# PE's branch around the further expert passes: the last position first, a copy of it behind the passes

## The reference

```
def moe_ffn(x, w_router, router_bias, w_gate, w_up, w_down):
    ...                                  # each token picks 2 of 16 experts, with weights
    h = silu(einsum("td,edf->tef", t, w_gate)) * einsum("td,edf->tef", t, w_up)
    h = h * gates[..., None]
    return einsum("tef,efd->td", h, w_down)
x = x + g2 * moe_ffn(h, ...)
y = rmsnorm(x, norm_final)
```

## Time and profile before

| | us |
|---|---|
| median of 3 runs | 634.96 (634.0 to 636.39) |
| profiled execution, its own time | 635.95 |
| span of the profiled execution, first to last instruction | 634.1 |
| PE busy (matmuls) | 566.3, 89% of the span |
| DVE busy | 247.6, 39% |
| ACT busy | 142.4, 22% |
| mean granted TensorE clock | 0.980 of full speed |

### The profile page before, as it was taken

One profiled execution on the slowest core, in us unless ns is written; L12 is line 12 of the kernel. 1 busy time (PEld: TensorE's weight loads), 2 busy tenths in 40 slices (PEclk: granted clock), 3 DMA queues, 4 the chain that ended last, 5 costly groups with the idle time before them and its releaser, 6 DMA issues.

```text
span 634.1 us, 13240 instructions
## 1 busy us (share of the span) xinstructions
PE 566.3 (89%) x5748; PEld 380.8 (60%) x5748; DVE 247.6 (39%) x541; ACT 142.4 (22%) x271; POOL 62.9 (10%) x93
## 2 busy tenths in 40 slices
PE   1978999999999999959998988999999977888784
PEld 0565553466667556646446787998777754555341
DVE  2463267888863673472035870101111100111026
ACT  1051245423213760101015211100111000111022
POOL 2009300000001210002000110010001000000021
PEclk9988999999999999989999999999999999998898
DMA  8959933030330191499968979999999999999652
GB/s 259 392 206 376 368 109 132 0 133 20 115 128 5 39 395 41 153 376 353 247 232 341 404 253 333 395 407 398 421 416 425 422 417 422 424 426 428 265 198 99
DMA packets 50460, 173.94 MB, mean 274 GB/s; under 512 B 6401, under 2 KB 11520, under 8 KB 44000
## 3 DMA queue, kind: packets, MB, share of 16 engines
q1 hardware_dynamic: 36672, 149.08, 61.3%
q0 software_dynamic: 5520, 16.78, 7.1%
q10 hardware_dynamic: 8207, 7.21, 3.5%
HBM read 160.59 MB, written 12.46 MB: 273 GB/s over the span
## 4 chain that ended last, share of the span: by engine, by line
PE 33%; DMA 12%; DVE 6%; issue 2%; SPq 2%; ACT 0%; DVEq 0%
PE psum L942 12%; DMA slot<-in_w_down 5%; DMA slot<-in_w_gate 5%; PE psum L832 5%; PE psum L934 5%; PE psum L931 3%; DMA xe<-h_rows,lst 2%; PE psum L839 2%; PE psum L1087 1%; PE psum L848 1%; PE psum L492 1%; SPq L1235 1%; DVE SEL L2347 1%; PE psum L962 1%; DVE slot L2486 1%
## 5 line engine op out<-in xcount | busy, mean ns | idle before, releaser
L580 PE MATMUL psum<-hT,slot 128*128 128x384 f32 x304 | 100.8, 489 | 0.0
L580 PEld LDWEIGHTS psum<-hT,slot 128*128 128x128 f32 x304 | 56.9, 190 | 38.2
L942 PE MATMUL psum<-slot,xeTa 128*32 128x256 f32 x1152 | 67.5, 384 | 6.7 <-DMA slot<-in_w_gate 4.6
L942 PEld LDWEIGHTS psum<-slot,xeTa 128*32 128x32 f32 x1152 | 43.1, 111 | 30.2 <-issue 10.3
L589 PE MATMUL psum<-slot,hT 128*128 128x512 f32 x96 | 42.3, 595 | 1.1 <-DMA slot<-in_w_in 1.1
L1734 ACT ACTIVATE he<-psum 128x256 f32<-128x256 f32 (+1 forms) x16 | 6.6, 411 | 125.5 <-PE psum L942 97.1
L2426 DVE TENSOR_TENSOR he<-he,psum 128x256 f32<-128x256 f32 (+1 forms) x16 | 7.3, 455 | 68.2 <-PE psum L942 50.7
L2444 DVE COPY ye<-psum 128x256 f32<-128x256 f32 (+1 forms) x15 | 6.9, 461 | 68.9 <-PE psum L942 43.7
L2430 DVE COPY heT<-psum 128x256 f32<-128x256 f32 (+1 forms) x16 | 7.3, 458 | 66.0 <-PE psum L962 66.0
L942 PE MATMUL psum<-slot,heT 128*32 128x256 f32 x512 | 31.1, 394 | 2.2 <-DMA slot<-in_w_down 1.1
L934 PE MATMUL psum<-slot,xeTa 128*32 128x128 f32 x288 | 32.7, 273 | 0.0
(11 more groups left out here) (487 smaller groups left out, 934.8 us busy)
## 6 DMA issues: line engine op xcount, KB each, us to landing
slot<-in_w_ada SPq DMA_DIRECT2D x12, 2048.0 KB, 13.3
slot<-in_w_gate SPq DMA_DIRECT2D x12, 2048.0 KB, 18.8
slot<-in_w_up SPq DMA_DIRECT2D x12, 2048.0 KB, 21.6
slot<-in_w_down SPq DMA_DIRECT2D x11, 2048.0 KB, 18.0
slot<-in_w_in SPq DMA_DIRECT2D x7, 2048.0 KB, 9.1
const<-in_w_gate SPq DMA_DIRECT2D x4, 1792.0 KB, 14.4
y_rows<-T POOLq DMA_DIRECT2D x11, 384.0 KB, 15.7
slot<-in_w_out SPq DMA_DIRECT2D x2, 2048.0 KB, 17.1
```

The source lines that it names most:

```text
L580: last = mm(o[:, 0:TOK], w[:, kt, tile(i)], hT[:, kt, :], start=(kt == 0), stop=(kt == KT - 1))
L942: last = mm(psum[32 * c:32 * c + 32, bank, 0:HALF], x(k, c % 2), w(k)[:, c // 2 * HALF:c // 2 * HALF + HALF], start=(k == 0), stop=(k == t ...
```

## The change

PE's code from `expert(E - 1)` to the end becomes a function, `last_expert`. It is called in two conditional blocks: in a new one, `If(more < 1)`, that follows position 14 directly, and at the end of the block `If(more > 0)`, behind the passes. PE's stream so holds the code of the last position twice. Nothing else is changed, and no other engine's stream.

```
+            def last_expert():
+
+                expert(E - 1)
+                pe.wait_ge(s["y15"], 2)
+                for turn in range(2):
...
+                pe.wait_ge(s["sums"], 2)
+                for j in range(NT):
+                    pe.wait_ge(s["zed"], j + 1)
...
             more = further(pe)
             expert(E - 2)
-
+            with pe.If(more < 1):
+                last_expert()
             with pe.If(more > 0):
                 pe.wait_ge(s["g_silu"], E)
...
                 for h in range(2):
                     carry(0, h)
-
-            expert(E - 1)
-            pe.wait_ge(s["y15"], 2)
-            for turn in range(2):
...
-            pe.wait_ge(s["sums"], 2)
-            for j in range(NT):
-                pe.wait_ge(s["zed"], j + 1)
...
+                last_expert()
```

More of the change, by code:

```diff
@@ L1101, in _ @@
             last.then_inc(s["sel_used"], 1)
+            def last_expert():
+                expert(E - 1)
+                pe.wait_ge(s["y15"], 2)
+                for turn in range(2):
+                    if turn:
+                        pe.wait_ge(s["sums"], 1)
+                    for j in range(NT):
+                        for c in range(2):
+                            h = (c + turn) % 2
+                            r = slice(c * SMALL, c * SMALL + SMALL)
+                            last = mm(psum[:, SUM[j][h], c * HALF:c * HALF + HALF], SELT[r, tile(j)],
+                                      Y15[min(j, 1)][r, h, :], start=False, stop=False, skip_group_check=True,
+                                      tile_position=(c * SMALL, 0))
+                    last.then_inc(s["sums"], 1)
+                pe.wait_ge(s["sums"], 2)
+                for j in range(NT):
+                    pe.wait_ge(s["zed"], j + 1)
+                    for h in range(2):
+                        last = mm(psum[:, SUM[j][h], :], ident, YG[0][:, j, h * CW:h * CW + CW], start=False, stop=True,
+                                  skip_group_check=True)
+                    last.then_inc(s["sums"], 1)
             more = further(pe)
             expert(E - 2)
+            with pe.If(more < 1):
+                last_expert()
             with pe.If(more > 0):
@@ L1133, in _ @@
                     carry(0, h)
-            expert(E - 1)
-            pe.wait_ge(s["y15"], 2)
-            for turn in range(2):
-                if turn:
-                    pe.wait_ge(s["sums"], 1)
-                for j in range(NT):
[L1141 to L1147, removed]
-            pe.wait_ge(s["sums"], 2)
-            for j in range(NT):
-                pe.wait_ge(s["zed"], j + 1)
[L1151 to L1154, removed]
+                last_expert()
         def steps(eng, name):
```

## The result

The changed kernel took 625.16 us (median of 4 runs, 624.55 to 626.31) against 634.79 us of the kernel before (4 runs, 634.0 to 636.39): 9.6 us less. The estimate of the ratio from these runs is 0.9873 with a 95% interval of 0.9843 to 0.9904, which is 6.1 to 10 us. The direction was forecast; the size was not: 5.3 us were forecast, and the range ended at 628.0. The profiled execution took 624.55 us, its span 622.6 against 634.1, so the pair of profiles is 11.5 us apart. The work is the same: PE is busy for 559.6 us against 566.3.

A forecast was written before the change was run, and what follows sets the result against it. PE was taken to bound the kernel, its jump ahead of position 15 lying on the chain. Idle time 3.1 plus clock 2.2 gave 5.3 us, 634.96 to 629.6; range 628.0 to 632.0.

The forecast's parts named there:

- step 1: Between PE's positions 14 and 15: moving the jump removes 3.23 us idle, adds 0.1 for the test; net 3.1 us.
- step 2: PE's carries and up matmuls of position 15 stay at full clock: 2.9 us in the profile, 2.2 for the median run.
- step 3: Behind position 14: the earlier work meets no late weights, VectorE jump or final rows; tightest slack 1.1 us.
- step 4: Behind PE's last matmul: the second jump is hidden under 8.4 us of cover; cost 0, uncovered 3.2 us.
- The idle time stays: Ahead of position 15: test or out-of-line body still stops PE, idle time and low clock remain; 634.9 us, chance 0.09.
- slower: Inside position 15: straight code isn't fetched ahead any more, a second stop adds 6.1 us; 641.1 us, chance 0.03.
- A late partner: Tail held by VectorE's jump, the weights or the gathers, losing about 2 us of gain; 631.6 us, chance 0.07.
- The clock falls later: Clock drops in the tail, at L1144, slowing the last L1152 matmuls by some 1.9 us; 631.5 us, chance 0.07.
- the cap of 7.1 us: Limit on the whole gain, from the final rows' 1.1 us of slack at VectorE; gives the low end, 627.9 us.

The follow-up runs named there:

- `swapped`: Changed kernel with its two blocks in the other order, so the jump is taken ahead of the last position; 633.27 us, ratio 0.9998 to the kernel before.
- `no_passes`: Changed kernel with the count's load, the tests and the passes dropped from PE's stream; 626.66 us, ratio 0.9874 to the kernel before.
- `after_again`: The changed kernel run once more, unaltered, beside the kernel before; 626.95 us against 633.38, ratio 0.9884.
- `late_gathers`: Changed kernel with GpSimd's six final gathers held back until PE has done position 15's down matmuls; 631.21 us.
- `plain_rows`: Changed kernel with SP loading consecutive final rows by six plain transfers in place of GpSimd's gathers; 622.72 us, ratio 0.9857 to the kernel before.
- `before_again`: The kernel before, unaltered, run again for a second profile; 633.19 us.
- `after_third`: The changed kernel run a third time, unaltered, against the kernel before; 622.9 us against 628.63, ratio 0.9926.

## Why the prediction was right or wrong

**The jump is the cause, and its place is what counts** (step 1): shown. It moved, and the idle time with it; `swapped` brought both back. The branch that falls through takes 0.09 us, where 0.1 was taken. The reading of the Trainium skill's page "Runtime: NRT & Kernel Launch", section "Instruction fetch mechanics", went the right way: a target some 880 instructions ahead was not at hand, for all the 2048 instructions that the page gives PE's memory, while some 25 ahead was. The prediction argued from a DMA packet in the idle time, which was right, and took it that no row shows a compare-and-branch; the branches' records were in the trace.

**The clock** (step 2): right in kind. In the pair of profiles it gave back 3.78 - 1.91 + 4.69 - 3.64 = 2.92 us, the very sum of the prediction. In the four profiles of the kernel before, the carries and up matmuls together took 2.85, 1.64, 2.66 and 1.67 us more than the 1.98 + 3.66 of full clock, 2.2 on average, which is what the prediction took for the median run. The idle time is 3.7 us on average, 0.6 more than step 1 had it, sized from one profile. 3.7 + 2.2 = 5.9 us, of which 5.6 are seen in the rest of the span, net of slow stretches and of other spells of low clock on either side, against 5.3 forecast: the sum of the steps holds for what lies behind position 14.

**What goes through** (step 3): all of it, in the first pair less the 2.4 us of the stretch in L1067, for which the prediction had no term. VectorE's jump, seen by its record (L2417, L2421 in the changed kernel), took 72 ns in both kernels, so that rival had no ground. VectorE waited for ScalarE nowhere ahead of a gated row; the up weights were in time.

**The second jump** (step 4): hidden. It ends 6.6 us ahead of the end, and without it (`no_passes`) no gain shows.

**The rivals.** "The idle time stays" and "slower" are out by the 89 ns record. "A late partner" didn't come. "The clock falls later" didn't come in the first profile, but in that of `after_again` (carries 2.89 us, L1067 4.39: 1.6 us more than at full clock) and in that of `no_passes`, for 2.7 us; `late_gathers` showed the same behind an idle time of 6.93 us at the end.

**The step that failed** is the base of the sum and of the range: "634.96 becomes 629.6", with "low end the cap of 7.1 us (627.9)". It puts at nothing, without a reason, what the executions do ahead of the change; only "the spread of the runs on top" was added, at the slow end. In the profiled pair 7.7 of the 11.5 us lie there, 3.65 of them from the slow start and 1.5 from the spell ahead of 578 us. The kernel before ran from 630.4 to 639.3 us in 23 executions on one chip, and its medians in the groups of runs lay between 628.4 and 634.8: 634.96, the median of three runs, lies above all of these. The gains at the medians were 9.6, 6.4, 5.7 and 3.8 us; the forecast of 5.3 lies inside them, the first result at their edge. Beside this, step 1's idle time was too small by 0.6 us on average.

How much of the 9.6 us is chance of the executions stays open, for only one of the first eight runs has a trace, and the profile of the kernel before is of one more execution. The intervals of the first ratio (0.9843 to 0.9904) and the last (0.9906 to 0.9966) don't meet, so scatter within one chip may not be all of it, and whether the gain itself differs from chip to chip isn't known. What the change does behind position 14 isn't in doubt, and the three later comparisons give 3.8 to 6.4 us for it.

## What to carry to other kernels

Where a branch stands on the engine that sets the end, let the case that runs fall through, and put the rare code behind it or at the end of the program, where another engine's work covers the jump; a copy of the code that both cases need costs nothing in the path. Look for the branch's own record in the trace, by its line, before arguing from idle time, and count what is queued behind it. Price an idle time of several us on TensorE with the matmuls behind it at half the clock, as here, and before setting a range, ask how far the executions of one kernel lie apart ahead of the change.

## What the runs showed that I had not expected

A jump on PE took 0.24, 1.03 and 3.9 to 6.1 us for some 25, 280 and 880 instructions, and the far one varied by 2.2 us between executions. Beyond that it didn't grow with the distance: over some 1230 instructions it took 5.3 us ahead of position 15 (`swapped`) and 3.3 to 3.8 behind the last matmul, in eight profiles. The end was always 2.4 to 2.9 us behind the start of one 16 KB packet; at the end of the program the packet went out 0.9 to 1.2 us into the jump, ahead of position 15 after 1.5 to 3.7. What delays it there stays open. VectorE's, over some 150 instructions by its code, took 0.07.

Within its last position PE had a slow stretch of some 1 to 2.6 us in eight of the ten profiles up to `plain_rows` (in `swapped` and `before_again` too, so it isn't the change's), and, but for 0.6 us at the end of `after_third`, in none of the six later ones, on two other chips. Its matmuls come there in pairs 0.7 us apart, or the last one's signal comes late: in `before_again` VectorE's product waited 3.07 us with PE's up matmuls done by their records. It began each time within the 7 us in which GpSimd issues the gathers, and lasted up to 1.8 us beyond them. What makes it stays open.
